# One fused three-block model on one core: the eight experts cut into 7 steps of 512 channels instead of 14 steps of 256

## The reference, cut to what matters

```python
# for each token: router logits, the two best experts, their softmax weights
# for each expert e, on the tokens that chose it:
#     gate = h @ moe_w_gate_3[e]     [1024, 3584]
#     up   = h @ moe_w_up_3[e]       [1024, 3584]
#     y    = (silu(gate) * up) @ moe_w_down_3[e]      [3584, 1024]
# x = x + sum over the two experts of weight * y, then a last RMS norm
```

## Time and profile before

| | |
|---|---|
| median of 3 executions | 2552.34 us (2552.05 to 2553.14) |
| the profiled execution, its own time | 2553.99 us |
| its span, from the first to the last instruction | 2552.1 us |
| PE matmuls busy | 2396.1 us, 94% of the span, 11965 instructions |
| DVE busy | 1965.9 us, 77% |
| ACT busy | 1442.5 us, 57% |
| DMA engines, share of the span | 74.0% on the weight queue |
| mean granted TensorE clock | 0.972 |

### The profile page before, as it was taken

One profiled execution on the slowest core, in us unless ns is written; L12 is line 12 of the kernel. 1 busy time (PEld: TensorE's weight loads), 2 busy tenths in 40 slices (PEclk: granted clock), 3 DMA queues, 4 the chain that ended last, 5 costly groups with the idle time before them and its releaser, 6 DMA issues.

```text
span 2552.1 us, 32705 instructions
## 1 busy us (share of the span) xinstructions
PE 2396.1 (94%) x11965; PEld 2001.3 (78%) x11965; DVE 1965.9 (77%) x1889; ACT 1442.5 (57%) x1418; POOL 17.6 (1%) x33
## 2 busy tenths in 40 slices
PE   4996999998999899799999969999999999999997
PEld 4865788867788798797887968888888888888886
DVE  6888778687687656675445748898989888888897
ACT  2553433546443454464434527777777777777775
POOL 0000000000000000000000000000000000000000
PEclk8997999999999899899999979999999999999998
DMA  8358699534598445455555429999999999999995
GB/s 326 124 173 297 226 317 321 187 121 164 167 329 300 145 163 187 131 170 173 188 183 165 165 83 331 361 340 350 350 340 359 333 366 334 366 334 366 331 368 180
DMA packets 435139, 651.79 MB, mean 255 GB/s; under 512 B 20688, under 2 KB 324432, under 8 KB 435040
## 3 DMA queue, kind: packets, MB, share of 16 engines
q1 hardware_dynamic: 432880, 643.59, 74.0%
q0 software_dynamic: 2160, 6.85, 0.8%
HBM read 649.32 MB, written 1.05 MB: 255 GB/s over the span
## 4 chain that ended last, share of the span: by engine, by line
PE 84%; DVE 9%; ACT 3%; issue 3%; DMA 1%; SPq 0%; DVEq 0%; POOL 0%; ACTq 0%
PE pair L1894 25%; PE pair L1896 25%; PE pair L1895 25%; DVE rest L1079 2%; PE pair L1929 2%; PE tb L2107 2%; DVE aw L1417 1%; ACT head L677 1%; DVE aw L1098 1%; PE pair L2017 1%; PE tb L1972 1%; DMA x<-in_x 1%; ACT aw L706 1%; DVE hT L1200 0%; DVE gat L1825 0%
## 5 line engine op out<-in xcount | busy, mean ns | idle before, releaser
L1079 DVE TENSOR_TENSOR rest<-raw,head 128x2048 fp32r<-128x2048 f32 x546 | 1249.2, 2292 | 296.2 <-ACT head L677 276.4
L677 ACT ACTIVATE head<-raw 128x2048 fp32r<-128x2048 f32 x546 | 1043.2, 1912 | 308.4 <-PE pair L1896 284.9
L1894 PE MATMUL pair<-head,hTh 128*128 128x512 f32 x1864 | 749.4, 402 | 21.2 <-DVE qkv L1509 6.8
L1896 PE MATMUL pair<-head,hTl 128*128 128x512 f32 x1864 | 731.5, 392 | 0.0
L1895 PE MATMUL pair<-rest,hTh 128*128 128x512 f32 x1864 | 730.6, 392 | 0.0
L1894 PEld LDWEIGHTS pair<-head,hTh 128*128 128x128 f32 x1864 | 352.5, 189 | 100.7 <-issue 16.3
L1896 PEld LDWEIGHTS pair<-head,hTl 128*128 128x128 f32 x1864 | 352.0, 189 | 75.0
L1895 PEld LDWEIGHTS pair<-rest,hTh 128*128 128x128 f32 x1864 | 353.0, 189 | 69.3 <-issue 1.5
L1894 PE MATMUL pair<-head,aTh 128*128 128x512 f32 x776 | 307.1, 396 | 2.6 <-issue 2.6
L1895 PE MATMUL pair<-rest,aTh 128*128 128x512 f32 x776 | 303.8, 392 | 0.0
L1896 PE MATMUL pair<-head,aTl 128*128 128x512 f32 x776 | 303.7, 391 | 0.0
(11 more groups left out here) (312 smaller groups left out, 1706.9 us busy)
## 6 DMA issues: line engine op xcount, KB each, us to landing
raw<-in_moe_w_gate SPq DMA_DIRECT2D x224, 512.0 KB, 6.0
raw<-in_moe_w_up SPq DMA_DIRECT2D x224, 512.0 KB, 7.1
raw<-in_moe_w_down SPq DMA_DIRECT2D x224, 512.0 KB, 6.7
raw<-in_w_in SPq DMA_DIRECT2D x152, 512.0 KB, 4.7
raw<-in_ada_w SPq DMA_DIRECT2D x96, 512.0 KB, 5.8
raw<-in_w_ffn_in SPq DMA_DIRECT2D x88, 512.0 KB, 5.5
raw<-in_w_ffn_out SPq DMA_DIRECT2D x44, 512.0 KB, 5.5
raw<-in_w_out SPq DMA_DIRECT2D x40, 512.0 KB, 4.8
```

Source lines behind the costliest of these rows:

```text
L677: act.activation(head[:, c.split, :], raw[:, c.raw, :], ACT.Copy).then_inc(heads_done, 1)
L1079: dve.tensor_tensor(rest[:, c.split, :], raw[:, c.raw, :], head[:, c.split, :].bitcast(F32), ALU.subtract).then_inc(rests_done, 1)
L1894: pe.matmul(out_, lh, rh, start=start, stop=False, skip_group_check=True)
L1896: return pe.matmul(out_, ll, rh, start=False, stop=stop, skip_group_check=True)
```

## The change

An expert has 7 steps of 512 channels with six chunks each, still 42 chunks. A chunk is now all gate (four tiles of 512 columns), all up, or all down (two tiles of 1024 columns). The two DMAs of a gate or up chunk move rows of 2 KB instead of 1 KB. Gate has bank 0 of `pair[0]`, up has bank 1, and steps no longer alternate. The hidden tile is 128 x 512, so it fills `aTh` and `aTl`, and the turned one-hots get a buffer `pslot` of their own. Order and waits change in each engine's program. The functions of the dense parts lose arguments and keep their instructions.

```diff
     STEPS3 = F3 // FB
-    PER = 3 * STEPS3
+    EB = 512
+    STEPSE = F3 // EB
+    PER = 6 * STEPSE
...
+        pslot = sb("pslot", [P, T, P], F32R)
...
-        pslot = aTh[:, :, P:S]
+        by_slots = lambda t: t[:, :, :].rearrange("p a s -> p (a s)").rearrange("p (k s) -> p k s", s=P)
+        aTh_e, aTl_e = by_slots(aTh), by_slots(aTl)
+        sg_e, act_e = qkv[:, 0, 0:EB], qkv[:, 1, 0:EB]
```

SP (one load function of the new two, and the order):

```diff
+                def wide(k, w, s, r):
                     c = At(MOE0 + k, it, PER)
+                    cols = slice(s * EB, (s + 1) * EB)
+                    load(c.place, c.placed(-RAW), landed[c.raw], [(slice(h * 2 * EB, (h + 1) * 2 * EB), w[:, bass.ds(e * KD + 4 * r + 2 * h, 2), cols])
+                                                                  for h in range(2)])
...
+                gate_and_up(0, 0)
+                for s in range(STEPSE - 1):
+                    gate_and_up(4 + 6 * s, s + 1)
+                    down(8 + 6 * s, s)
+                down(PER - 2, STEPSE - 1)
```

ACT:

```diff
+            def expert_step(c, s):
+
+                make_head(c.next(2))
+                make_head(c.next(3))
+                turned_head(s)
+                make_head(c.next(4))
+                silu_wide(c.next(1), s + 1)
+                for d in (5, 6, 7):
+                    make_head(c.next(d))
...
                 make_head(at.next(2))
-                make_head(at.next(3))
                 act.wait_ge(sem("picks_turned"), it + 1)
                 act.activation(slot_weight, tb[1][:, 256:257], ACT.Copy)
...
+                make_head(at.next(3))
+                make_head(at.next(4))
+                silu_wide(at.next(1), s0)
+                make_head(at.next(5))
+                for s in range(STEPSE - 1):
+                    expert_step(at.next(4 + 6 * s), s0 + s)
+                turned_head(s0 + (STEPSE - 1))
+                make_head(at.next(PER))
                 act.wait_ge(sem("slots_ready"), it + 1)
                 act.wait_ge(sem("y_half"), it + 1)
                 y_head(0)
                 gathered_head(it + (window + 2))
                 act.wait_ge(chunk_used, at.next(PER - 1).count())
                 y_head(1)
+                make_head(at.next(PER + 1))
```

DVE:

```diff
+            def gated_wide(c, s):
+                dve.wait_ge(sem("silu_ready"), s + 1)
+                dve.wait_ge(chunk_used, c.count())
+                dve.tensor_tensor(act_e, sg_e, EXPERT_BANKS[0][:, 1, :], ALU.mult).then_inc(act_ready, 1)
+
+            def expert_step(c, s):
                 make_rest(c.next(2))
                 make_rest(c.next(3))
+                turned_rest(s)
                 make_rest(c.next(4))
+                make_rest(c.next(5))
+                gated_wide(c.next(3), s + 1)
+                make_rest(c.next(6))
+                make_rest(c.next(7))
...
+                for d in (2, 3, 4, 5):
+                    make_rest(at.next(d))
+                gated_wide(at.next(3), s0)
+                for s in range(STEPSE - 1):
+                    expert_step(at.next(4 + 6 * s), s0 + s)
+                turned_rest(s0 + (STEPSE - 1))
+                make_rest(at.next(PER))
                 gathered_rest(it + (window + 2), lambda: y_rest(it, 0))
                 y_rest(it, 1)
+                make_rest(at.next(PER + 1))
                 for t in range(T):
                     dve.wait_ge(sem("scattered"), it * 2 + (t + 1))
```

PE (a `wide` chunk is 4 x `three` into one bank; `half_down` is 6 matmuls of one half of the output columns):

```diff
+            def gate(c, s, r):
+                if r == 0:
+                    pe.wait_ge(sem("silu_ready"), s)
+                wide(c, EXPERT_BANKS[0][:, 0, :], r)
+            def up(c, s, r):
+                if r == 0:
+                    pe.wait_ge(act_ready, s)
+                wide(c, EXPERT_BANKS[0][:, 1, :], r)
+            def turn_wide(s):
+                pe.wait_ge(act_ready, s + 1)
+                pe.wait_ge(atl_ready, s)
+                for k in range(4):
+                    ins = pe.transpose(tb[0][:, k * P:(k + 1) * P], act_e[:, k * P:(k + 1) * P], ident)
+                ins.then_inc(turned, 1)
...
             def expert_last_down(c, s):
-                pe.wait_ge(rests_done, c.placed())
                 pe.wait_ge(atl_ready, s + 1)
+                pe.wait_ge(rests_done, c.next(1).placed())
+                half_down(c, 0, 0, False, False)
+                half_down(c.next(1), 1, 0, False, True).then_inc(sem("y_half"), 1)
+                half_down(c, 0, 1, False, False).then_inc(chunk_used, 1)
+                half_down(c.next(1), 1, 1, False, True).then_inc(chunk_used, 1)
+            def expert_step(c, s, first):
+                gate(c, s + 1, 0)
+                turn_wide(s)
+                gate(c.next(1), s + 1, 1)
+                up(c.next(2), s + 1, 0)
+                up(c.next(3), s + 1, 1)
+                expert_down(c.next(4), s, first)
...
                 pe.wait_ge(sem("xe_rest"), it + (window + 1))
-                gate_up(at, s0, 0, (0,), 0, s0 - 1, EXPERT_BANKS)
+                gate(at, s0, 0)
                 pe.wait_ge(sem("weights_ready"), it + 1)
...
-                gate_up(at.next(1), s0, 1, (0,), 0, None, EXPERT_BANKS)
+                gate(at.next(1), s0, 1)
+                up(at.next(2), s0, 0)
+                up(at.next(3), s0, 1)
                 pe.wait_ge(sem("scatter_added"), it * 2 + 2)
...
+                turn_wide(s0 + (STEPSE - 1))
                 gather(it + (window + 2))
-                expert_last_down(at.next(PER - 1), s0 + (STEPS3 - 1))
+                expert_last_down(at.next(PER - 2), s0 + (STEPSE - 1))
```

More of the change, by code:

```diff
@@ L1526, in dense_step @@
                 mods_now()
-                turned_rest(s, T)
+                turned_rest(s)
                 feed(c + 4)
@@ L2085, in mix, with gate_up @@
                 linear_by_tiles(f"wout{k}.1", (1, 3, 5)[k], x if k < 2 else xn, sums=((0, 4),) if k == 0 else ())
-            def gate_up(c, s, half, tiles_, b, wait_for, banks, used=True):
+            def gate_up(c, s, half, tiles_, wait_for, banks, used=True):
                 if half == 0:
@@ L2100, in gate_up, with turn_hidden @@
                     ins.then_inc(chunk_used, 1)
-            def turn_hidden(s, nt):
+            def turn_hidden(s):
                 pe.wait_ge(act_ready, s + 1)
                 wait(pe, atl_ready, s)
-                for t in range(nt):
+                for t in range(T):
                     for k in range(2):
@@ L2283, in gather, with wide @@
                 ins.then_inc(sem("gather_done"), 1)
+            def wide(c, bank_, r):
+                pe.wait_ge(rests_done, c.placed())
+                for k in range(4):
+                    wcols = slice(k * EB, (k + 1) * EB)
+                    ins = three(bank_, hTh[:, 4 * r + k, 0:P], hTl[:, 4 * r + k, 0:P], head[:, c.split, wcols], rest[:, c.split, wcols],
+                                r == 0 and k == 0, r == 1 and k == 3)
+                ins.then_inc(chunk_used, 1)
+            def gate(c, s, r):
+                if r == 0:
+                    pe.wait_ge(sem("silu_ready"), s)
+                wide(c, EXPERT_BANKS[0][:, 0, :], r)
@@ new lines, in up, with half_down @@
+            def up(c, s, r):
[5 more added lines that the diff above has]
+                pe.wait_ge(atl_ready, s)
+                for k in range(4):
+                    ins = pe.transpose(tb[0][:, k * P:(k + 1) * P], act_e[:, k * P:(k + 1) * P], ident)
+                ins.then_inc(turned, 1)
+            def half_down(c, r, n, start, stop):
+                for k in range(2):
+                    wcols = slice(k * D + n * NT, k * D + (n + 1) * NT)
+                    ins = three(pair[1][:, n, :], aTh_e[:, 2 * r + k, :], aTl_e[:, 2 * r + k, :], head[:, c.split, wcols],
+                                rest[:, c.split, wcols], start and k == 0, stop and k == 1)
+                return ins
@@ L2285, in expert_last_down, with expert_down @@
+            def expert_down(c, s, first):
+                pe.wait_ge(atl_ready, s + 1)
+                for r in range(2):
+                    pe.wait_ge(rests_done, c.next(r).placed())
+                    half_down(c.next(r), r, 0, first and r == 0, False)
+                    half_down(c.next(r), r, 1, first and r == 0, False).then_inc(chunk_used, 1)
             def expert_last_down(c, s):
-                pe.wait_ge(rests_done, c.placed())
                 pe.wait_ge(atl_ready, s + 1)
-                for n in range(2):
-                    for k in range(2):
-                        wcols = slice(k * D + n * NT, k * D + (n + 1) * NT)
-                        ins = three(pair[1][:, n, :], aTh[:, k, 0:P], aTl[:, k, 0:P], head[:, c.split, wcols],
-                                    rest[:, c.split, wcols], False, k == 1)
-                    ins.then_inc(chunk_used if n == 1 else sem("y_half"), 1)
+                pe.wait_ge(rests_done, c.next(1).placed())
[3 more added lines that the diff above has]
+                half_down(c.next(1), 1, 1, False, True).then_inc(chunk_used, 1)
```

121 lines of the change are left out of this document (51 added, 70 removed).

## The result

The changed kernel takes 2571.09 us (median of 4, 2569.51 to 2572.68) against 2552.56 for the kernel before: ratio 1.0073, 95% interval 1.0055 to 1.009, slower by 18.5 us. The forecast was 2565.2, with a range of 2557 to 2580. The direction, the place and the mechanism hold; about 6 us in the profiled execution come from something that the prediction held to be unlikely, a lower clock. The profiled execution is the slowest of the four, 2572.68 us.

The account below looks back on a forecast made before the run. PE was taken to bound the experts, idle only at passages. Per passage -0.81 + 2.35 + 0.10 - 0.07 = +1.57 us, seven times +11.0, plus 1.92 at the end: +12.9, about 2565.2 us, range 2557 to 2580.

Parts of the forecast that it names:

- What bounds, steps, transposes: Experts: PE bounds them and waits only at passages; longer steps cost nothing, transposes give -0.07 us an expert.
- the cover of 0.9 us: Inside the steps: copies, rests and products each are ready 0.9 us or more before PE needs them.
- rival A: Inside the steps: the cover goes and PE waits 0.3 us in 48 steps, +14 us, 2580; chance 0.07.
- The transposes and the banks: Inside the steps: fewer, longer transpose groups give -0.07 us an expert; contiguous strips and a bank each give nothing.
- Weights: Weight loads in the experts: 2 KB rows give 0 us, since no engine waits for a DMA.
- Scatter: Passage between experts: 8 scatter matmuls take 2.57 us against 3.38, -0.81 us, with gathered tokens handled under the longer last down.
- The moved rest: Passage: chunk 43's rest now stands ahead of the additions, so token weights come late and PE idles 2.35 us more.
- Rivals C and D: Passage: C, new wait half as long, about 2556, chance 0.07; D, wait stays covered, 2546, 0.07 shared with DMA rival.
- The next late one: After the passage: the first hidden tile is late for the four transposes, +0.10 us.
- The end: Behind the last expert: additions start at 14.51 instead of 12.59 and everything after follows, +1.92 us.
- rival B: Passage: the clock falls in the new idle stretch, 7 x 2.7 = +19 us, 2584; chance 0.04.
- The sum: Whole kernel: seven passages at +1.57 us, +11.0, and +1.92 at the end make +12.9 us.

Follow-up runs that it names:

- e3: Changed kernel with gate and up chunks loaded in rows of 1 KB instead of 2 KB: 2570.58 us, ratio 1.0075.
- e6: Kernel before, steps of 256, with additions moved out of the passage and the rest of chunk 44 made before the next one-hots: 2548.82 us, ratio 0.9984.
- e5: Changed kernel with additions spread over the following expert, rest of chunk 43 behind the token weights, first expert's early rest not made before the loop: 2544.24 us, ratio 0.9966.
- e1: Changed kernel with DVE's rest of chunk 43 behind additions and token weights, and the first expert's rest no longer made before the loop: 2551.70 us, ratio 1.000.
- e4: Kernel before with only the head and rest of chunk 43 moved behind the second output half, as in the changed kernel: 2570.51 us, ratio 1.0071.
- e2: Changed kernel with 8 extra unread matmuls between chunk 42 and the wait for the token weights: 2566.41 us, ratio 1.0056.
- e8: Changed kernel with 4 extra unread matmuls between chunk 42 and the wait for the token weights: 2565.33 us, ratio 1.0049.

## Why the prediction was right, and where it was short

**What bounds, steps, transposes.** Right. PE has no idle time inside the steps of 512 either, and the cover of 0.9 us held; rival A did not happen. The transposes and the banks gave nothing that can be told apart.

**Weights.** Right, and e3 shows it apart: 0 us. The rule in the Trainium skill, Perfetto Trace Analysis, section DMA Optimizations, agrees with the trace in what it says of the DMA engines (5.3 us to landing instead of 7.0) and gives no time here, since no engine waits for a landing in the expert stretch.

**Scatter.** Forecast 2.57 us for its 8 matmuls, measured 2.54 (3.38 before). This gain of the wide steps is real; e6 lacks it, and e5 has it. With the waits at chunk 44, which e5 has and e6 has not, the two are 2.0 us apart over the eight experts.

**The moved rest.** Forecast 2.35 us of idle time ahead of the one-hots, measured 2.29; 14.51 for the start of the additions after chunk 39, measured 14.41. e1 takes it away and gets back 16.2 of the 18.5 us of the expert stretch, e4 puts it alone into the kernel before and gets the new time. So the cause is shown from both sides: it is the place of the rest of chunk 43 (and of its head on ACT), not the size of the steps. Rivals C and D, a shorter or a covered wait, fell.

**The next late one.** Forecast 0.10 us in front of the first transposes; the profile has PE's next matmul at 1671.57 - 1671.24 = 0.33 behind the last one, where 0.23 is its usual distance. Right where the clock stays; in the four passages with a fall the wait there is 0.5 us, which the prediction did not have.

**The end.** Forecast +1.92, measured +1.91.

**The clock.** This is the step that was short: rival B, which the prediction gave 0.04. It argued from one row that after 2.40 us of idle PE the clock stayed at 1.00, so that 2.4 us "are too few for that". One stretch that did not fall was taken for a rule. In the changed kernel the clock fell behind four of seven like stretches, in e3 too; in e4 also behind four of seven, with 1.6 us of idle time. What decides between a fall and none is open. The price was also off: 1.57 us for each fall and not 2.7, since the clock is back after 3.5 us. The Trainium skill, page TensorE: Matmul & The Clock Gate, Part 1, says that an idle array goes back to the lower clock; the trace agrees at four of the seven passages (0.54 behind 2.2 us of idle time at 1786.78), and at the other three the clock stayed at 1.00. Without the falls the changed kernel takes what e2 takes, 2566.4, and the forecast of 2565.2 would have been right to 1.2 us. The waits are 10.3 us against 11.0 forecast and owe nothing to luck; that the time lies in the range with four falls that the forecast left out is luck, since the range was laid out for other rivals.

**The sum.** 12.9 us forecast, 18.7 measured between the profiles (18.5 between the medians): 10.3 for seven periods of waits (11.0 forecast), 1.9 for the end, 6.3 for the clock, 0.2 for the start.

## What to carry to other kernels

Where one engine has a queue written out by hand, ask at every seam which item another engine waits for, and put nothing in front of it that is not needed first. The seam ahead of the loop is one too: a rest of 2.3 us in the middle of the last norm stands in front of the router in both kernels, and without it, in e1 and e5, the router's matmuls start 2.4 us earlier than in the changed kernel. Here one 2.3 us instruction in front of two additions and a small product cost more than all the gains of larger tiles. Work that nobody needs soon (the additions) belongs into the steps in which the engine has time to spare, even if it is only 0.9 us at a time in pieces. And price an idle stretch of PE with its clock as well: a wait of 1.6 to 2.3 us was followed at four of seven passages, in each of three profiles, by 3.5 us at about half speed.

## What the runs showed of the hardware

- The granted clock fell behind idle stretches of PE of 2.3 us (changed kernel, e3) and 1.6 us (e4) at four of seven passages each, and at none where the stretches are 1.2 us or less (e1, e2, e5 to e8, before). Stretches alike in length and in the work around them fell or did not.
- Eight matmuls whose result nobody reads, put into the wait, were worth 4.7 us of the median (2571.1 to 2566.4, from two comparisons with the kernel before, at 2552.6 and 2552.0).
- Rows of 2 KB instead of 1 KB brought a 512 KB load from 7.0 to 5.3 us at about the same demand (379 and 368 GB/s).
